# The order of work where a large expert begins: gathered tokens before the first weights, the small expert's return between gate pieces

## The reference

```python
def moe_swiglu(h, router, w13, w2):
    logits = (h @ router).astype(F32)
    top_val, top_idx = lax.top_k(logits, TOP_K)        # 2 of 8
    weights = jax.nn.softmax(top_val, axis=-1)
    combine = jnp.einsum('blk,blke->ble', weights,
                         jax.nn.one_hot(top_idx, N_EXPERTS, dtype=F32)).astype(h.dtype)
    out = jnp.zeros_like(h)
    for e in range(N_EXPERTS):
        out = out + combine[..., e:e + 1] * swiglu(h, w13[e], w2[e])
    return out
```

## Time and profile before

| | us |
|---|---|
| median of 3 runs | 2239.25 (2238.32 to 2239.54) |
| the profiled execution | 2238.85, span 2237.1 |
| PE busy | 2151.9 (96%) |
| DVE busy | 1177.3 (53%) |
| ACT busy | 913.6 (41%) |
| expert loop | from about 1347 to 2223 |

### The profile page before, as it was taken

One profiled execution on the slowest core, in us unless ns is written; L12 is line 12 of the kernel. 1 busy time (PEld: TensorE's weight loads), 2 busy tenths in 40 slices (PEclk: granted clock), 3 DMA queues, 4 the chain that ended last, 5 costly groups with the idle time before them and its releaser, 6 DMA issues.

```text
span 2237.1 us, 56085 instructions
## 1 busy us (share of the span) xinstructions
PE 2151.9 (96%) x24686; PEld 1584.8 (71%) x24686; DVE 1177.3 (53%) x1581; ACT 913.6 (41%) x1196; POOL 179.7 (8%) x181
## 2 busy tenths in 40 slices
PE   8999999999999999999999899999999999989997
PEld 5677667688888747888888778853885388448843
DVE  2544695522233386666666539830982198119802
ACT  4322012522222294555555337711771177127700
POOL 2000371100000012200000100000000000000000
PEclk9999999999999999999999999999999999999999
DMA  8566306333322341111110258999999999999997
GB/s 292 189 222 238 122 1 201 116 97 94 94 94 94 102 138 35 35 35 35 35 35 26 89 214 312 365 358 406 404 406 387 406 405 405 398 405 405 405 394 286
DMA packets 220597, 491.19 MB, mean 220 GB/s; under 512 B 14631, under 2 KB 107711, under 8 KB 220095
## 3 DMA queue, kind: packets, MB, share of 16 engines
q1 hardware_dynamic: 218974, 482.44, 58.3%
q10 hardware_dynamic: 1442, 6.06, 0.8%
HBM read 486.37 MB, written 2.10 MB: 218 GB/s over the span
## 4 chain that ended last, share of the span: by engine, by line
PE 81%; DMA 5%; DVE 5%; SPq 4%; ACT 3%; issue 2%; POOL 0%; DVEq 0%; ACTq 0%
PE bank L1778 14%; PE bank L1809 7%; PE bank L1863 5%; DMA expert_w<-in_moe_w_dram 4%; PE bank L1245 4%; PE bank L1246 4%; PE bank L1247 4%; SPq L919 4%; PE bank L1151 2%; PE bank L1122 2%; PE bank L1413 2%; PE bank L1123 2%; PE bank L1124 2%; PE bank L1377 2%; PE bank L1263 2%
## 5 line engine op out<-in xcount | busy, mean ns | idle before, releaser
L3247 DVE TENSOR_TENSOR w_low<-expert_w,w_high 128x1792 fp32r<-128x1792 f32 (+1 forms) x192 | 384.7, 2023 | 49.3 <-ACT w_high L2420 48.5
L2420 ACT CAST w_high<-expert_w 128x1792 fp32r<-128x1792 f32 (+1 forms) x192 | 325.0, 1700 | 113.2 <-PE bank L1778 80.9
L1863 PE MATMUL bank<-expert_w,arena 128*64 128x448 f32 x1024 | 198.9, 541 | 1.0 <-DMA expert_w<-in_moe_w_dram 0.9
L1863 PEld LDWEIGHTS bank<-expert_w,arena 128*64 128x64 f32 x1024 | 72.1, 137 | 117.3 <-issue 116.2
L1778 PE MATMUL bank<-w_high,xg_high 128*128 128x448 f32 x512 | 149.2, 373 | 5.4 <-DVE xg_low L3237 5.2
L1778 PE MATMUL bank<-w_low,xg_high 128*128 128x448 f32 x512 | 147.7, 370 | 0.0
L1778 PE MATMUL bank<-w_high,xg_low 128*128 128x448 f32 x512 | 147.3, 369 | 0.0
L1245 PE MATMUL bank<-u_high,ring_high 128*128 128x512 f32 x352 | 139.2, 396 | 2.0 <-DVE u_low L2888 2.0
L1246 PE MATMUL bank<-u_low,ring_high 128*128 128x512 f32 x352 | 139.0, 395 | 0.0
L1247 PE MATMUL bank<-u_high,ring_low 128*128 128x512 f32 x352 | 138.4, 393 | 0.0
L2467 ACT ACTIVATE arena<-bank 128x448 f32<-128x448 f32 x16 | 8.7, 543 | 260.0 <-PE bank L1863 260.0
(11 more groups left out here) (454 smaller groups left out, 4206.0 us busy)
## 6 DMA issues: line engine op xcount, KB each, us to landing
expert_w<-in_moe_w_dram SPq DMA_DIRECT2D x128, 1792.0 KB, 18.0
expert_w<-in_moe_w_dram SPq DMA_DIRECT2D x32, 2048.0 KB, 17.6
arena<-in_mod_w_dram SPq DMA_DIRECT2D x48, 1024.0 KB, 8.2
expert_w<-in_moe_w_dram SPq DMA_DIRECT2D x32, 1536.0 KB, 17.7
arena<-in_ffn_w_dram SPq DMA_DIRECT2D x44, 512.0 KB, 5.1
arena<-in_hy_w_in_dram SPq DMA_DIRECT2D x12, 1024.0 KB, 5.4
arena<-in_rw_w_rkv_dram SPq DMA_DIRECT2D x48, 256.0 KB, 2.9
arena<-in_ffn_w_dram SPq DMA_DIRECT2D x11, 1024.0 KB, 4.9
```

Of the source, the lines that this page charges most:

```text
L1863: last = pe.matmul(b[hd(v), 0:EH], small_x[:, k, :], w[:, kk, v * EH:v * EH + EH], start=(k == 0), stop=(k == KT - 1))
L2420: act.copy(high_piece(kind, n), piece(kind, ering[q % ERN], n // 2, n % 2))\
L3247: dve.tensor_tensor(piece(kind, low[s], n // 2, n % 2), piece(kind, ering[s], n // 2, n % 2), high_piece(kind, n).bitcast(F32), ALU.subtract)\
```

## The change

In the large expert's first chunk, three orders change, and the lists of steps with them. ACT writes the gathered tokens' high digits before it casts the first gate piece. DVE does the tokens' low digits first, then low digits of gate pieces 0 and 1, then the small yield, then pieces 2 and 3. PE starts with gate pieces 0 and 1, then does the return products, then gate pieces 2 and 3. Nothing is added or removed.

```diff
@@ _expert_steps
-        pe += ["small_combined"] * (c == 0) + pieces(f"gate{c}") + [f"turned{c - 1}"] * (c > 0) + pieces(f"up{c}")
+        pe += pieces(f"gate{c}", [0, 1]) + ["small_combined"] * (c == 0) + pieces(f"gate{c}", [2, 3])
+        pe += [f"turned{c - 1}"] * (c > 0) + pieces(f"up{c}")
-        act += [f"high_gate{c}_0"] + ["xg_high"] * (c == 0) + pieces(f"high_gate{c}", range(1, PIECES))
+        act += ["xg_high"] * (c == 0) + pieces(f"high_gate{c}")
-        dve += ["small_yield"] * (c == 0) + [f"low_gate{c}_0"] + ["xg_low"] * (c == 0)
-        dve += pieces(f"low_gate{c}", range(1, PIECES)) + ["small_added"] * (c == 0)
+        dve += ["xg_low"] * (c == 0) + pieces(f"low_gate{c}", [0, 1]) + ["small_yield"] * (c == 0)
+        dve += pieces(f"low_gate{c}", [2, 3]) + ["small_added"] * (c == 0)
@@ PE, large
                     if c == 0:
+                        step(pe, "expert_vectors", "xg_low", couple)
+                        hidden_products("gate", 0, couple, [0, 1])
                         step(pe, "expert_vectors", "small_yield", couple)
                         settle(pe)
                         combine((6, 7, 2, 3), of_small).then_inc(sem("expert_products"), 1)
-                        step(pe, "expert_vectors", "xg_low", couple)
+                        hidden_products("gate", 0, couple, [2, 3])
                     else:
                         step(pe, "expert_copies", f"silu{c - 1}", couple)
-                    hidden_products("gate", c, couple)
+                        hidden_products("gate", c, couple)
@@ ACT, large
-                    high_digits("gate", c, couple, [0])
                     if c == 0:
                         act.wait_ge(sem("first_expert"), 2)
                         step(act, "expert_products", "small_gathered", couple - 1)
                         copy_gathered().then_inc(sem("expert_copies"), 1)
-                    high_digits("gate", c, couple, range(1, PIECES))
+                    high_digits("gate", c, couple)
@@ DVE, large
-                step(dve, "expert_products", f"small_down{EC - 1}_1", couple - 1)
-                step(dve, "expert_vectors", f"small_h{EC - 1}", couple - 1)
-                yield_small().then_inc(sem("expert_vectors"), 1)
                 for c in range(EC):
-                    low_digits("gate", c, couple, [0])
                     if c == 0:
                         step(dve, "expert_copies", "xg_high", couple)
                         gathered_low().then_inc(sem("expert_vectors"), 1)
-                    low_digits("gate", c, couple, range(1, PIECES))
+                    low_digits("gate", c, couple, [0, 1])
+                    if c == 0:
+                        step(dve, "expert_products", f"small_down{EC - 1}_1", couple - 1)
+                        step(dve, "expert_vectors", f"small_h{EC - 1}", couple - 1)
+                        yield_small().then_inc(sem("expert_vectors"), 1)
+                    low_digits("gate", c, couple, [2, 3])
```

More of the change, by code:

```diff
@@ L1766, in of_small, with hidden_products @@
                 return pickT[hd(half), tt, :], small_rows[hd(half), :]
-            def hidden_products(kind, c, item):
+            def hidden_products(kind, c, item, ns=range(PIECES)):
                 b0 = 0 if kind == "gate" else 2
-                for n in range(PIECES):
+                for n in ns:
                     step(pe, "expert_vectors", f"low_{kind}{c}_{n}", item)
```

## The result

| | before | after |
|---|---|---|
| median | 2239.39 us (12 runs, 2237.31 to 2243.77) | 2245.39 us (12 runs, 2241.77 to 2252.56) |
| ratio | | 1.0027, 95% interval 1.0016 to 1.0038 |
| profiled execution | span 2237.1 | span 2250.8 |
| gather's end to the span's end | 2237.1 - 1346.92 = 890.2 us | 2250.8 - 1356.15 = 894.7 us |

The changed kernel is slower by 6.0 us by the medians, 3.6 to 8.5 us by the interval. 2244.2 was forecast, range 2240.5 to 2247.8.

A forecast was written before the change was run, and what follows sets the result against it. PE was taken to bound the loop up to about 1475 us, DMA after that. First expert +4.8 and later heads +0.1 gave +4.9 us, so 2244.2 us with the median at 2239.25; range 2240.5 to 2247.8.

The forecast's parts named there:

- First expert: First large expert, where PE sets the pace: +4.8 us in sum, bounds 1.6 and 7.8.
- start of PE: First large expert: first gate matmul later, with the table load behind the gather: +1.2 us, or -0.1 were the load earlier.
- Products in line: Return products between gate pieces 1 and 2 no longer fill PE's wait: +1.9 us, bounds 1.7 and 3.7.
- Clock: First large expert: PE's clock falls to half behind 6.2 us of idle time: +1.7 us, bounds 0 and 2.9.
- the 3 that would have spoken against it: Sign of error: the first small expert starting less than 3 us later; 4.8 us later was expected.
- The sags: Lower weight-load rates where later large experts end, 5.2 us in all; a change over 2 us would speak against the prediction.
- rival 1: First expert: table load stays ahead of the gather's wait, or no clock fall: 2242.4 to 2242.9 us, chance 0.23.
- Later heads: Starts of the three later large experts: earlier first matmul against in-line products and clock: +0.1 us in sum, bounds -2.6 and +3.5.
- The factor of 0.7: Later large experts: 1.5 us of lateness cost 1.0 us of period, so PE time there counts at 0.7.
- Rival 2: Earlier start of the three later heads decides, worth 5.2 us at most: 2238.2 us, chance 0.08.
- rival 4: The first expert's delay is swallowed by slack of PE or buffers, end unchanged: 2239.3 us, chance 0.05.
- rival 3: Longer slow-clock stretch in the first expert and at one or two later heads: 2247.5 us, chance 0.12.

The follow-up runs named there:

- the filled wait: Changed kernel with six float32 matmuls (results unused) on PE once, ahead of the loop, in its wait at the first head: ratio 1.0026, 2244.09 us.
- the run with the twelve: Kernel before with twelve float32 matmuls of 512 columns (results unused) on PE once, between the gather and the expert loop: ratio 1.0035, 2247.97 us.

## Why the prediction was right

**First expert: +4.8 forecast, +4.7 measured.** Lateness went from 15.0 to 19.7, the distance from 216.9 to 221.6. By terms: start of PE +1.2 forecast, 6.25 - 4.94 = +1.3 measured, with the table load behind the gather as the order in the earlier trace rows said; taking it away gave 1.3 back. Products in line 1.9 forecast, 1370.95 - 1369.03 = 1.92 measured, and 2.0 when nothing else was left. Clock 1.7 forecast; 1.6 by the filled wait. That a late PE counts in full here is shown by the run with the twelve, 6.9 of 7.1. One such pair is uncertain by about 1 us: four executions with the same lateness of 15.0 had distances of 216.0, 216.7, 216.9 and 217.8. But over the first heads of all thirteen executions, with lateness from 15.0 to 22.1, the straight line through the pairs has a slope of 0.97, and none lies more than 1.1 us off it. The small expert started 4.1 us later, less than the 4.8 forecast and above the 3 that would have spoken against it: the three sequences of 48 matmuls behind the first gate ran 0.3, 0.2 and 0.1 us faster than before (see the end). The sags changed by 1.3 us at most, and PE waited neither for the small yield nor for the first low digits of up.

Two things in these terms were not as forecast. The clock's 1.7 was one stretch of 3.3 us wholly over matmuls; it was a stretch of 6.8 us, half of which ran out while PE was still waiting. That the price came out the same is luck: where all of such a stretch lay over matmuls, in the run with four matmuls at each head, the first gate matmul came at the same 6.25 us and lateness was 21.1, 1.4 more. And the 0.26 us of wait that the prediction takes off the gate pieces is in no row: before, the four take 9.91 us, 2.48 each, and up follows within 0.15 us. The sum doesn't hang on it. Nor can the ends of the range be added up as told: rival 1 with both of its terms gives 2241.2, and the upper bounds of the products and of the clock together 2247.2.

**Later heads: +0.1 forecast, -0.2 measured** (distances -1.7, +0.8, +0.6). Lateness: -1.0, +0.6, +0.6 forecast, -0.9, +2.0, +0.7 measured. The third is the clock's doing: there the slow stretch lay on eight pairs of matmuls (1800.07 to 1806.24 above), where 1 to 3.3 us of it had been forecast. A spread of this kind was in the bounds, and is seen in the same kernels from one head to the next.

**The factor of 0.7 was the weak step**, and that the later heads came out near zero is luck: -0.7, +0.4 and +0.4 were forecast, -1.7, +0.8 and +0.6 measured, and the errors cancel. The factor came from two points. In all thirteen profiled executions (twelve kernels, one of them twice) the relation has a knee (three later heads each, 39 pairs):

| lateness | distance of second and third | of fourth |
|---|---|---|
| 14.7 to 16.0 | 218.3 to 218.8 | 233.8 to 234.4 |
| 16.5 to 17.4 | 218.4 to 219.5 | 233.9 to 234.6 |
| 17.9 to 19.0 | 219.4 to 220.8 | 235.3 to 236.4 |
| 20.0 to 20.6 | 221.9 to 222.2 | 237.1 to 237.4 |

Below about 17 us little or nothing is gained, above it each microsecond costs about one. An estimate says why: a large and a small expert are 88.1 MB of weights, which at the 405 GB/s of the stretches between the sags is 217.5 us. The distances of the second and third couple can't fall much below that, and the shortest are 218.3. The kernel before stood at the knee with its third and fourth couple (16.5) and above it with its second (18.0). That is why tokens first with the table load ahead, 3.3, 1.1 and 1.8 us earlier than the kernel before at its later heads, shortened the distances by 1.6, 0.9 and 0.1 us only, and not by the 4 to 5 that I expected of it. Rival 2 (the sags' 5.2 us are to be had) falls with this: even with lateness 15.3 at all later heads, these gave only 2.2 and 2.6 us in the two executions, 1.8 of it in each at the second head, where the clock fall on gate matmuls went away together with the table load.

Of the other rivals, rival 1 described what the table load's removal does, but not this kernel; rival 4 is out; rival 3's longer slow stretch occurs (first and third head; in the first it is half hidden, in the run with four fillers it isn't) and makes the upper part of the range real. The median's 6.0 against the loop's 4.5 I can't tell apart from the spread ahead of the loop.

On the Trainium skill's rule of the long idle gaps (TensorE: Matmul & The Clock Gate, HAM oscillation): behind one wait of 6.25 us the clock fell and cost 1.6 us of lateness, and with 5.2 us of this wait filled it stayed up, so this trace agrees. But a long gap was not needed: in the kernel before it fell at all three later heads, where the longest gap was 2.3 us. The Trainium skill (ScalarE: Activation LUTs, What ACT_TABLE_LOAD costs) gives a drain of 1.38 us beside the load; here the token cast starts 0.01 us behind the load's 1.28 (1356.34, 1357.63), and taking the load off saved 1.3, so no more than the load shows.

## What to carry to other kernels

When a loop's body is reordered, work out the first iteration by itself: what hides behind a transfer in every later turn has nothing to hide behind in the first, and here that turn was the only one in which PE's time counted in full from the first microsecond. Work that really runs in an engine's idle time is free (the fillers at the loop's turn began too late for that), moved out of it it costs all of its time, and the idle time left behind may cost clock as well. Where a transfer sets the pace, ask how late the engine may be before the transfer feels it: on the early side of that point, next to nothing that you save is paid out.

## What the runs showed of the hardware that I had not expected

- PE takes at least some 2.1 us to go round the loop: at a later head the return products start 2.1 to 2.3 us behind the landing where they stand first (seventeen of eighteen heads in six executions; one at 3.5, where PE was late), though the small yield is done at 1.6, and the filler, which waits for nothing new, starts after 2.22, 2.07 and 3.65 us of "issue". With the tokens first and the table load ahead, PE was free 1.1 us before the second landing and the yield done at 0.5 behind it, and the products still started only at 2.2, after 3.32 us of "issue" (row below). So the return would hardly have come earlier by a faster yield. What PE does in this time the profile doesn't show.

```profile
1574.54 1.99 PE L1758 MATMUL bank<-arena 64*128 64x512 f32 x8 [3.32 <-issue]
```

- Float32 matmuls ahead of the gate matmuls kept the granted clock at 1.00 behind them when little idle time was left: 10.5 us of them with none, 5.2 with 1.1 us, 3.4 with 1.5 us. 3.4 us of them with 2.8 us of idle time did not. The same sequence doesn't always end the same way: the kernel before and the run with the twelve have six later heads with a gap of 2.3 us, the products and a second gap. The clock fell by the first gap at two of them, behind the second at three, and at one, with gaps of 2.30 and 2.41 us, not at all.
- The same sequence of 48 gate or up matmuls at full clock took 9.91 us in most places and 9.61 us in a few, in the same execution. I have no cause for it.
